# A group of four tokens weighed behind the second token's broadcast of the next group instead of behind the first

## The reference

```
top_s, pos = lax.top_k(cand, PEER_TOPK)              # 8 heads x 16 experts per token
g = jax.nn.softmax(top_s, -1).astype(xc.dtype)
h = jax.nn.gelu(jnp.einsum('thkd,td->thk', eu[eidx], xc), approximate=False)
return jnp.einsum('thk,thkd->td', g * h, ev[eidx])
```

## Time and profile before

| | |
|---|---|
| median of 3 runs | 3236.44 us (3234.24 to 3240.46) |
| the profiled execution's own time | 3230.94 us |
| its span | 3229.1 us |
| granted TensorE clock, mean | 0.773 of full speed |
| TensorE busy | 2497.8 us (77%) |
| VectorE busy | 1904.0 us (59%) |
| GpSimd busy | 970.9 us (30%) |
| expert rows moved | 768 asks, 805.36 MB of 1021.45 MB |

### The profile page before, as it was taken

One profiled execution on the slowest core, in us unless ns is written; L12 is line 12 of the kernel. 1 busy time (PEld: TensorE's weight loads), 2 busy tenths in 40 slices (PEclk: granted clock), 3 DMA queues, 4 the chain that ended last, 5 costly groups with the idle time before them and its releaser, 6 DMA issues.

```text
span 3229.1 us, 34224 instructions
## 1 busy us (share of the span) xinstructions
PE 2497.8 (77%) x11680; PEld 1295.8 (40%) x11680; DVE 1904.0 (59%) x6025; ACT 494.3 (15%) x1069; POOL 970.9 (30%) x968
## 2 busy tenths in 40 slices
PE   7879986597899978737979987776888657776565
PEld 5768882053355544303535543111678101121111
DVE  3668987746544456785444445555437865555555
ACT  2151121013322210001112221000412000000000
POOL 0830002248322222212772223333000333333332
PEclk7989996587799988857979997565899556555656
DMA  8607737798899988866989998999330989999997
GB/s 311 242 30 293 298 150 278 315 376 300 329 394 389 363 325 352 321 255 266 390 317 378 416 406 341 404 405 379 134 115 13 373 321 406 394 397 376 401 398 303
DMA packets 147887, 1021.45 MB, mean 316 GB/s; under 512 B 18816, under 2 KB 20352, under 8 KB 28032
## 3 DMA queue, kind: packets, MB, share of 16 engines
q0 software_dynamic: 110592, 805.36, 62.9%
q1 hardware_dynamic: 30496, 201.31, 15.9%
q10 hardware_dynamic: 6624, 12.59, 1.0%
HBM read 1010.27 MB, written 8.91 MB: 316 GB/s over the span
## 4 chain that ended last, share of the span: by engine, by line
PE 43%; DMA 21%; DVE 17%; POOL 8%; issue 6%; ACT 3%; ACTq 0%; SPq 0%; DVEq 0%; POOLq 0%
DMA ring<-in_peer_uv,eT 20%; PE PS L1219 11%; PE PS L904 7%; DVE ring L2110 6%; POOL ring L739 5%; PE PS L1237 5%; PE PS L839 4%; PE PS L982 3%; PE PS L1112 3%; PE PS L909 2%; POOL mix L625 2%; PE PS L1063 1%; PE PS L929 1%; DVE ring L1648 1%; ACT uT L1301 1%
## 5 line engine op out<-in xcount | busy, mean ns | idle before, releaser
L2110 DVE CUSTOM_DVE_ANT_0 ring<-ring,PS 128x512 f32<-128x512 f32 x1536 | 994.6, 685 | 777.4 <-PE PS L1237 399.5
L739 POOL DMA_INDIRECT ring<-in_peer_uv,eT x768 | 729.4, 950 | 2126.2 <-PE PS L1219 1351.7
L1237 PE MATMUL PS<-xr,onesb 3*128 3x512 bf16 x1536 | 643.6, 484 | 421.6 <-DVE hcol L2110 364.7
L1219 PE MATMUL PS<-ring,zcol 128*32 128x512 f32 x3072 | 579.5, 894 | 107.9 <-DVE zcol L2120 105.6
L1237 PEld LDWEIGHTS PS<-xr,onesb 3*128 3x128 bf16 x1536 | 114.9, 96 | 1033.9 <-DVE hcol L2110 550.1
L1219 PEld LDWEIGHTS PS<-ring,zcol 128*32 128x32 f32 x3072 | 102.8, 142 | 406.7 <-issue 226.6
L1577 ACT ACTIVATE ge<-hdot 128x4 f32<-128x4 f32 x192 | 39.5, 206 | 1408.0 <-DVE hdot L2115 1378.6
L904 PE MATMUL PS<-uT,W 128*128 128x256 f32 x1024 | 249.1, 392 | 7.5 <-issue 7.5
L904 PEld LDWEIGHTS PS<-uT,W 128*128 128x128 f32 x1024 | 193.1, 194 | 65.9 <-issue 39.8
L1648 DVE CUSTOM_DVE_ANT_0 ring<-ring 128x1024 f32<-128x1024 f32 x160 | 205.7, 1326 | 8.3 <-DMA ring<-in_w_rows 3.5
L839 PE MATMUL PS<-uT,W 128*128 128x256 f32 (+1 forms) x720 | 172.0, 394 | 18.0 <-ACT uT L1301 18.0
(11 more groups left out here) (268 smaller groups left out, 2381.6 us busy)
## 6 DMA issues: line engine op xcount, KB each, us to landing
ring<-in_w_rows SPq DMA_DIRECT2D x40, 1024.0 KB, 8.0
W<-in_w_in SPq DMA_DIRECT2D x30, 1024.0 KB
W<-in_w_gate SPq DMA_DIRECT2D x16, 1408.0 KB
W<-in_w_gate SPq DMA_DIRECT2D x16, 1280.0 KB
W<-in_w_gate SPq DMA_DIRECT2D x16, 1152.0 KB
ring<-in_w_q SPq DMA_DIRECT2D x16, 1024.0 KB, 12.6
W<-in_w_out SPq DMA_DIRECT2D x12, 1024.0 KB
xr<-xrows ACTq DMA_DIRECT2D x768, 6.0 KB
```

What stands on the lines that cost most here:

```text
L739: pool.indirect_dma_start(ring[:, slot, :], None, (peer_uv0, peer_uv1)[b.l], bass.IndirectOffsetOnAxis(eT[:, f % 2, t:t + 1], 0)).then_inc ...
L1219: last = T.matmul(PS[k * NR:(k + 1) * NR, (6 + h) * 512:(7 + h) * 512], zcol[:, g % 2, k, NR - 1 - at:2 * NR - 1 - at], ring[:, slot, D + ...
L1237: T.matmul(bank(x_bank(q, n) + h), onesb[32 * k:32 * k + 3, :], xr[32 * k:32 * k + 3, g % 2, h * 512:(h + 1) * 512], start=True, stop=True)\
L2110: V.tensor_tensor_reduce(out=u_half, in0=u_half, in1=bank(x_bank(q, n) + h), scale=1.0, scalar=0.0, op0=ALU.mult, op1=ALU.add, accum_out=h ...
```

## The change

In TensorE's list, `weigh(g - 1)` stands behind the broadcast of the second token of group g (k == 1) instead of behind the first (k == 0).

```
                                 .then_inc(xb_s, 1)
-                        if k == 0 and g % NR:
+                        if k == 1 and g % NR:
                             weigh(g - 1)
                         if k == GRP - 1 and g % NR == NR - 1:
                             weigh(g)
```

## The result

The changed kernel takes **3340.32 us** in the median of four runs (3338.89 to 3358.15), the kernel before 3237.03 us in its four. The ratio is 1.0342 (95% interval 1.0317 to 1.0368): 3.4% or 103 us slower. Forecast were 3284 us in a range of 3248 to 3314. The sign was right, the forecast rise of 48 us was less than half of what came, and the time lies outside the range.

A forecast was written before the change was run, and what follows sets the result against it. The prediction took the DMA rate to bound the lone stretches, with no engine full. It summed 42 (lone stretches) + 0 (last stretch) + 6 (mixed stages) = 48 us, 3284 us from 3236.4, range 3248 to 3314.

The forecast's parts named there:

- The lone stretches are bound by the rate of the DMA engines: Three stretches of expert tokens alone: DMA share 1.00 or 1.01, about 400 GB/s, some 10.5 us a group.
- `weigh(A)` starts 1.8 us after B0 lands: Lone stretches with one pair of banks: `weigh(A)` waits behind B1's broadcast and starts 3.0 us later than before.
- The cover of 1.9 us: Lone stretches: asks of C come 5.1 us before the queue empties, less 3.2 before data flow, leaving 1.9 a group.
- The loop of 11.5 us: Lone stretches, one pair of banks: B0's landing to C0's takes 11.5 us against 10.5; 0.9 taken, +42 us for 47 groups.
- 7.98 us: Upper end for an ask's time to landing, from an ask into a full queue; the loop would be 13.7 us.
- 0 us for the last stretch: Second tile of `LAT1`, two pairs of banks: `weigh` doesn't move in time, so 31 groups cost 0 us.
- +6 us for the mixed stages: The other 108 moved calls: gain and loss nearly cancel, +6 us, with -22 and +32 as ends.
- The mixed stages pay too: Rival: each of 108 mixed-stage calls costs 0.5 us, 54 us on top of 42, giving 3332 us; chance 0.08.
- The queue stays full: Rival: a dry queue delivers within 4.7 us of the ask, two lone stretches cost nothing, 3236 to 3246 us; chance 0.12.
- TensorE gains: Rival: up to 42 us of `zcol` waits outside the last stretch vanish, about 3215 us; chance 0.08.
- The clock: Rival: a higher clock in the lone stretches shrinks the loop by 1.7 us to 9.8, about 3242 us; chance 0.04.
- The signs: Expected profile: two lone stretches at 11.2 to 11.6 us a group, last at 10.6; wrong if mixed stages move over 20 us.

The follow-up runs named there:

- e11_half_weigh: The kernel before, with the second half of the columns left out of `weigh` (output lacks them), so asks come earlier: 3186.19 us, ratio 0.9861.
- e3_ask_late: The kernel before, with only GpSimd's asks of group C also waiting for the broadcast of B1, `weigh` unmoved: 3315.44 us, ratio 1.0274.
- e13_ask_dot1: The kernel before, with the asks of C also waiting until VectorE has dotted B1, nothing else moved: 3425.95 us, ratio 1.0603.
- e14_ask_dot2: The kernel before, with the asks of C also waiting until VectorE has dotted B2, nothing else moved: 3680.49 us, ratio 1.1370.
- e5_ahead: The kernel before, with `weigh` one token later in TensorE's list but still ahead of B1's broadcast: 3238.04 us, ratio 1.0015.
- e10_by_token: The kernel before, with `weighed` counted for each token instead of each group, so slots are released one by one: 3232.75 us, ratio 0.9998.
- e8_first: The kernel before, with `weigh` of A moved ahead of B0's broadcast in TensorE's list: 3339.26 us, ratio 1.0334.
- e7_half_after: The changed kernel, with each token's gather bringing 4 KB a row instead of 8: 3133.79 us, ratio 0.9689 to the kernel before.

## Why the prediction was wrong, step by step

- **The lone stretches are bound by the rate of the DMA engines.** Right for the kernel before: e11_half_weigh asks earlier and gains 0.03 us a group.
- **`weigh(A)` starts 1.8 us after B0 lands.** Right: 1.89 in the mean, 1.90 in the group shown.
- **The cover of 1.9 us.** Wrong: it was close to 0, as e3_ask_late shows. It was worked out up to the landing of B3, "the asks of C come 5.1 us before the queue is empty". The sixteen engines finish their shares one after the other. In the changed kernel B3's dot comes 2.55 us after the ask, but in the second us after the ask only 7.8 of the 16 engines are busy, in the mean over 20 groups; in the kernel before it is 15.5 or more at every time. The step decided little, as the sum went by the loop.
- **The loop of 11.5 us, of which 0.9 was taken for each group.** The loop was right: 1.89 + 3.59 + 0.30 + 5.78 = 11.56 in the `CTX0` stretch with a pace of 11.6. The shading from 1.0 to 0.9 for engines that don't run dry together was the wrong way. It cost 27.8 / 26 = 1.07 us a group there, and 26.3 / 21 = 1.25 in `LAT1`, where C0's dot comes 6.03 after the ask. That is 54 us instead of 42. The 5.78 us of the earlier trace rows was the right row to go by. That 7.98 us "can't hold for a dry queue" was too sure: on the nearly dry queue of e13_ask_dot1 it is 7.2 to 8.4 in 16 of 20 groups. By the Trainium skill ("DMA: Bandwidth & Descriptors", section "Anatomy of one DMA — SWDGE (gpsimd) path") an estimate for 1 MB is 4.4 us; the traces don't agree: in the changed kernel and e14_ask_dot2 the sixteen parts of a gather end 4.5 to 5.8 us after the ask, and its dot starts 5.3 to 6.1 after it.
- **0 us for the last stretch.** Right, and for the reason given: -0.9 us over 26 groups, and VectorE waits for rows instead of for B1's broadcast.
- **+6 us for the mixed stages.** This is the step that failed: 52 us. "TensorE does the same work in another order. It loses where B0 isn't dotted when the broadcast of B1 is reached" named the mechanism, and the sum then set its size as nearly equal to the gain at `zcol`, with no row for the loss. The gain was 14.8 us and the loss 43.6, and TensorE's work itself took 24 us longer at the lower clock, a term that the sum didn't have. I had looked at the gate products for the price, where TensorE is full; 19.6 us of the loss arise by group 24, before the gate products, where VectorE's selection work makes the dots late. In the gate products themselves another 17.0 come by group 40, of which 7.2 are given back by group 48. The second sentence that failed is that a later ask hides in these stages because "a dot is mostly late for VectorE's own work and not for its data": its waits for data rose from 109.5 to 181.2 us.
- **The rivals.** "The mixed stages pay too" named the price of 0.5 us a call, 54 us, and the time of 3332; it had a chance of 0.08. Its reason, asks late into stages without cover, is a part of what the runs showed; another is TensorE's standing before B1's broadcast. "The queue stays full" fell: C0's dot comes 5.8 us after the ask, not 4.7 or less. "TensorE gains" fell with the result, and e5_ahead shows that the move alone, without the new dependency, gains nothing either. "The clock" as a gain in the lone stretches fell, it stayed at 0.58 and 0.59; that it could fall in the mixed stages was no rival, and it did, from 0.83 to 0.81.
- **The signs.** The windows at 11.6 and 11.7 us with shares of 0.94 and 0.93, and L1219's wait for `zcol` at 21.6 us in the whole span instead of 105.6, were as forecast or within 0.1 us of it. "The span up to 1985 us longer by less than 10" was not: 45.5. So the last sign of being wrong, "if the mixed stages move by more than 20 us", is the one that came.

No kernel of this series that does the whole work beats the kernel before: e5_ahead and e10_by_token can't be told from it.

## What to carry over

An instruction that frees a buffer should stand in its engine's list ahead of anything that waits for a younger transfer, but not so far ahead that it waits itself with ready work behind it: e8_first lost as much that way. Ask of every moved instruction what the one now in front of it waits for: e5_ahead and the changed kernel differ by one broadcast, and by 100 us. A queue at a DMA share of 1.00 says nothing about spare time; whether an ask may come later is found by making it later by a known amount, and here 0.74 us were already too much. And a gain and a loss on the same engine can't be taken to cancel because both look small: price each by itself, from rows of the stage in which it is largest.

## What the hardware showed that I had not expected

- A gather of 1 MB is over when the last of its sixteen parts is. With the queue nearly but not quite dry (e13_ask_dot1) the last part came about 2.5 us after the others in 16 of 20 groups, and the changed kernel, which asks 1.0 us later, was faster: 11.58 us a group instead of 12.22. The cause is open.
- A gather's dot starts 5.7 to 5.8 us after its ask for 1 MB (e14_ask_dot2, the changed kernel) and 4.3 us for 0.5 MB (e7_half_after): half of the bytes take off a quarter of the time. Four asks in a row are 1.24 us apart (0.94 and a pause of 0.30).
- The same matmuls keep TensorE busy 24 us longer in the mixed stages of the changed kernel, at a granted clock of 0.81 instead of 0.83, in a window in which it also waits 22 us more.
